# Scan products and low parts inside the passes, three attention steps for a pair of heads

## What is computed

```python
h = rmsnorm(x, norm_mix_w); proj = h @ w_in                # columns: z, xBC, dt, q, k, v, f
xbc = silu(causal_dwconv(xBC)); y_ssm = ssd_chunked(...)   # 16 heads of 64, 4 chunks of 128
y_ssm = rmsnorm(y_ssm * silu(z), ssm_norm_w)
q, k = rmsnorm per head; log_f = log_sigmoid(f + bias)     # 16 attention heads of 64
y_att = rmsnorm(forgetting_attention(q, k, v, log_f))      # causal, 4 blocks of 128 queries
x = x + concat(y_ssm, y_att) @ w_out
x = x + hierarchical_moe(rmsnorm(x))                       # 32 experts, top 1 group, top 2 in it
```

## Time and profile before

| | before |
|---|---|
| median of 3 runs | 728.06 us (727.43 to 728.72) |
| the profiled execution | 728.84 us |
| its span, first to last instruction | 727.1 us |
| mean granted TensorE clock, share of 2.4 GHz | 0.977 |
| busy: PE, DVE, ACT, POOL | 681.2, 392.7, 292.3, 148.9 us |
| moved by DMA | 162.78 MB |
| passes 20 to 35, window 137.12 to 264.00: PE busy, DVE busy | 123.67, 102.22 of 126.88 us |
| passes 44 to 51, window 304.70 to 418.10: PE busy, DVE busy | 109.89, 83.23 of 113.40 us |

### The profile page before, as it was taken

One profiled execution on the slowest core, in us unless ns is written; L12 is line 12 of the kernel. 1 busy time (PEld: TensorE's weight loads), 2 busy tenths in 40 slices (PEclk: granted clock), 3 DMA queues, 4 the chain that ended last, 5 costly groups with the idle time before them and its releaser, 6 DMA issues.

```text
span 727.1 us, 10707 instructions
## 1 busy us (share of the span) xinstructions
PE 681.2 (94%) x3850; PEld 467.0 (64%) x3850; DVE 392.7 (54%) x850; ACT 292.3 (40%) x659; POOL 148.9 (20%) x178
## 2 busy tenths in 40 slices
PE   8999999999999999999989999989999978887984
PEld 7878888777777888766656788877434323332542
DVE  6865778778879647777787654471222211121221
ACT  5934533564554636655665433221212111121200
POOL 2300010123312120012342142010132331122331
PEclk9999999999999999999999999989999989999998
DMA  8333345416346243290020069699999999999993
GB/s 295 101 106 116 98 152 162 132 70 174 112 121 170 63 146 117 78 356 1 30 88 1 3 226 421 257 368 355 409 420 415 404 411 402 420 419 414 416 397 109
DMA packets 61160, 162.78 MB, mean 224 GB/s; under 512 B 14184, under 2 KB 25604, under 8 KB 49840
## 3 DMA queue, kind: packets, MB, share of 16 engines
q1 hardware_dynamic: 49120, 144.64, 53.3%
q0 software_dynamic: 6880, 9.02, 4.2%
q10 hardware_dynamic: 5104, 8.39, 3.1%
HBM read 157.67 MB, written 20.28 MB: 245 GB/s over the span
## 4 chain that ended last, share of the span: by engine, by line
PE 31%; SPq 18%; DMA 3%; DVE 2%; issue 2%; ACT 1%; POOL 0%; POOLq 0%; DVEq 0%; ACTq 0%
SPq L401 6%; SPq L435 6%; SPq L449 5%; PE bank L1779 4%; PE bank L1373 4%; PE bank L1375 4%; PE bank L1374 4%; PE bank L1601 3%; DMA s_dn<-in_w_expert_down_dram 3%; PE bank L1808 3%; PE bank L1586 3%; PE bank L1577 2%; PE bank L1750 2%; SPq L443 1%; PE bank L1644 1%
## 5 line engine op out<-in xcount | busy, mean ns | idle before, releaser
L1779 PE MATMUL bank<-s_gu,s_xgT 128*64 128x512 f32 x352 | 84.7, 637 | 18.2 <-DMA s_gu<-in_w_expert_up_dram 18.2
L281 DVE TENSOR_TENSOR s_wl<-s_raw,s_wh 128x512 fp32r<-128x512 f32 x105 | 91.1, 913 | 11.9 <-ACT s_wh L994 11.5
L994 ACT ACTIVATE s_wh<-s_raw 128x512 fp32r<-128x512 f32 x120 | 72.8, 628 | 41.7 <-DMA s_raw<-in_w_in_dram 17.8
L1373 PE MATMUL bank<-s_wh,s_hTh 128*128 128x512 f32 x192 | 78.7, 410 | 0.0
L1779 PEld LDWEIGHTS bank<-s_gu,s_xgT 128*64 128x64 f32 x352 | 28.8, 146 | 73.2 <-issue 73.2
L1375 PE MATMUL bank<-s_wh,s_hTl 128*128 128x512 f32 x192 | 75.2, 391 | 0.0
L1374 PE MATMUL bank<-s_wl,s_hTh 128*128 128x512 f32 x192 | 74.8, 390 | 0.0
L1289 ACT ACTIVATE s_sg<-bank,s_slot_scale 128x256 f32<-128x256 f32 x16 | 7.6, 475 | 150.6 <-PE bank L1779 115.5
L1808 PE MATMUL bank<-s_dn,s_hidT 128*64 128x512 f32 x256 | 58.7, 599 | 2.0 <-DVE s_hidT L2347 1.6
L2347 DVE COPY s_hidT<-bank 128x256 f32<-128x256 f32 x16 | 6.8, 424 | 96.0 <-PE bank L1788 96.0
L2380 DVE SCALAR_TENSOR_TENSOR s_yrow<-bank,s_slot_scale,s_xg 128x512 f32<-128x512 f32 x30 | 21.2, 747 | 47.1 <-PE bank L1808 47.1
(11 more groups left out here) (307 smaller groups left out, 1402.3 us busy)
## 6 DMA issues: line engine op xcount, KB each, us to landing
s_dn<-in_w_expert_down_dram SPq DMA_DIRECT2D x28, 1024.0 KB, 28.9
s_gu<-in_w_expert_gate_dram SPq DMA_DIRECT2D x26, 1024.0 KB
s_gu<-in_w_expert_up_dram SPq DMA_DIRECT2D x24, 1024.0 KB, 28.8
s_raw<-in_w_in_dram SPq DMA_DIRECT2D x88, 256.0 KB, 4.0
s_raw<-in_w_out_dram SPq DMA_DIRECT2D x32, 256.0 KB, 3.7
s_gu<-in_w_expert_up_dram SPq DMA_DIRECT2D x12, 512.0 KB
s_decay_rows<-decay_rows SPq DMA_DIRECT2D x4, 1024.0 KB, 4.7
s_gu<-in_w_expert_gate_dram SPq DMA_DIRECT2D x8, 512.0 KB
```

The costliest lines, as they stand in the source:

```text
L281: eng.tensor_tensor(low, full, high.bitcast(F32), ALU.subtract).then_inc(sem(f"{what}_low_{low_engine(what, i)}"), 1)
L994: act.activation(wh[:, i % HL, :], raw[:, i % RAW, :], ACT.Copy).then_inc(sem("w_high"), 1)
L1373: pe.matmul(dst, ah, bh, start=start, stop=False)
L1779: last = pe.matmul(ps[j][r, :].rearrange("p (w f) -> p w f", w=2), m["xgT"][:, j, k, r], gu[:, half, :, k, :], start=(k == 0), stop=(k == ...
```

## The change

It has two parts. In the scan, `cb(0)` stands behind tile 4 of pass 21 instead of tile 1; `diag(c, 0)` and `diag(c, 1)` behind tiles 2 and 4 of the chunk's third pass instead of 1 and 3; `diag(c, 2)` and `diag(c, 3)` behind tiles 1 and 3 of the fourth pass instead of together ahead of it. The seven lows that VectorE made behind `y_add(c, 1)` are split: one ahead of `y_add(c, 1)`, three behind it, one between `qk_sum` and `qk_scale` of the fourth pass, two behind `state_keep`. In the attention, the last two query blocks of a pair (256 and 128 keys) become one step: 24 steps (`NEV`), with two row blocks in one bank, one P tile and one store, and still 54 tiles to spread them over.

```diff
-T_QK, T_P, T_END = T_X + 18, T_X + 34, T_X + 98
+T_QK, T_P, T_END = T_X + 18, T_X + 34, T_X + 82
...
+NEH = 3
+NEV = NEH * NHP
...
-    first, end = ((max(0, i) * NSTEP + 53) // 54 for i in ((n - N_SO) * KC + k, (n - N_SO) * KC + k + 1))
+    first, end = ((max(0, i) * NEV + 53) // 54 for i in ((n - N_SO) * KC + k, (n - N_SO) * KC + k + 1))
...
+        def steps_of(e):
+            hp, part = divmod(e, NEH)
+            return (TC * hp + part,) if part < NEH - 1 else (TC * hp + part, TC * hp + part + 1)
+        def spot(v):
+            step, par = divmod(v, 2)
+            hp, back = divmod(step, TC)
+            return 2 * (NEH * hp + min(back, NEH - 1)) + par, 2 * P if back == TC - 1 else 0
...
-                    if i == 1 and k == 1:
+                    if i == 1 and k == 4:
                         cb(0)
-                    if i >= 2 and i % 4 == 2 and k in (1, 3):
-                        diag(i // 4, k // 2)
+                    if i >= 2 and i % 4 == 2 and k in (2, 4):
+                        diag(i // 4, k // 2 - 1)
+                    if i >= 2 and i % 4 == 3 and k in (1, 3):
+                        diag(i // 4, 2 + k // 2)
...
                 if step == 1:
                     if c:
                         y_off(c, 1)
-                    diag(c, 2)
-                    diag(c, 3)
...
-            def p_transpose(step):
-                for v in (2 * step, 2 * step + 1):
+            def p_transpose(e):
+                for u in (2 * e, 2 * e + 1):
+                    pe.wait_ge(sem("p_scaled"), units_of(u)[-1] + 1)
...
             for i in range(16):
+                late = [r for r in slots_after(N_QK + i - 1)[4:] if low_engine("w", r) == "dve"] if i % 4 == 3 else []
                 qk_sum(i)
+                if late:
+                    weight_low(dve, late[0])
                 qk_scale(i)
...
                 if i % 4 == 2:
+                    soon = [r for r in slots_after(N_QK + i)[:4] if low_engine("w", r) == "dve"]
+                    for r in soon[:1]:
+                        weight_low(dve, r)
                     y_add(c, 1)
+                    for r in soon[1:]:
+                        weight_low(dve, r)
                 if i % 4 == 3 and c < TC - 1:
                     state_keep(c, 0)
                     state_keep(c, 1)
-                lows_after(N_QK + i)
+                for r in late[1:]:
+                    weight_low(dve, r)
+                if i % 4 != 2:
+                    lows_after(N_QK + i)
...
-                        if s + 2 < NSTEP:
-                            row_max(2 * s + 4)
-                            row_max(2 * s + 5)
+                        ahead = steps_of(s + 2) if s + 2 < NEV else ()
+                        if ahead:
+                            row_max(2 * ahead[0])
+                            row_max(2 * ahead[0] + 1)
                         pt_store(2 * s + 1)
-                        if s + 1 < NSTEP:
+                        if len(ahead) > 1:
+                            row_max(2 * ahead[1])
+                            row_max(2 * ahead[1] + 1)
+                        if s + 1 < NEV:
                             p_scale(s + 1)
```

More of the change, by code:

```diff
@@ L1567, in y_sums @@
                 last.then_inc(sem("sums_done"), 1)
-            def scores(step):
-                pair = (2 * step, 2 * step + 1)
-                for v in pair:
-                    h, hp, qb, n = unit(v)
-                    if v >= 3:
-                        pe.wait_ge(sem("max_known"), v - 2)
-                    r = slice((h % 2) * HD, (h % 2 + 1) * HD)
-                    pe.matmul(ps[4 + v % 3][:, 0:n], qT[r, hp, qb * P:(qb + 1) * P], kT[r, hp, 0:n], start=True, stop=True)\
-                        .then_inc(sem("s_done"), 1)
@@ L1580, in p_transpose, with scores @@
-            def p_transpose(step):
-                for v in (2 * step, 2 * step + 1):
-                    h, hp, qb, n = unit(v)
-                    pe.wait_ge(sem("p_scaled"), v + 1)
-                    t_read(pe, T_P + v - 2)
-                    for kb in range(qb + 1):
-                        last = pe.transpose(tbank(T_P + v)[:, kb * P:(kb + 1) * P], p_tile(v)[:, kb * P:(kb + 1) * P], ident[:])
+            def scores(e):
+                for step in steps_of(e):
+                    for v in (2 * step, 2 * step + 1):
+                        h, hp, qb, n = unit(v)
+                        u, off = spot(v)
+                        if u >= 3 and off == 0:
+                            pe.wait_ge(sem("max_known"), units_of(u - 3)[-1] + 1)
+                        r = slice((h % 2) * HD, (h % 2 + 1) * HD)
+                        pe.matmul(s_bank(v), qT[r, hp, qb * P:(qb + 1) * P], kT[r, hp, 0:n], start=True, stop=True)\
+                            .then_inc(sem("s_done"), 1)
@@ new lines, in p_transpose @@
+            def p_transpose(e):
+                for u in (2 * e, 2 * e + 1):
+                    pe.wait_ge(sem("p_scaled"), units_of(u)[-1] + 1)
+                    t_read(pe, T_P + u - 2)
+                    for v in units_of(u):
+                        h, hp, qb, n = unit(v)
+                        off = spot(v)[1]
+                        for kb in range(qb + 1):
+                            last = pe.transpose(tbank(T_P + u)[:, off + kb * P:off + (kb + 1) * P], p_tile(v)[:, kb * P:(kb + 1) * P], ident[:])
@@ L1624, in _ @@
                     if n == N_AO - 1 and k == 0:
-                        pv(NSTEP - 1)
+                        pv(NEV - 1)
             def x2_transpose(c):
```

127 lines of the change are left out of this document (71 added, 56 removed).

## The result

| | before | after |
|---|---|---|
| median of 8 runs each | 728.84 us (727.43 to 730.52) | 732.00 us (730.78 to 734.49) |
| the profiled execution, its span | 728.84, 727.1 us | 731.53, 729.8 us |
| tile 2 of pass 20 to the first score product | 154.54 us | 164.12 us |
| first score product to the first product of pass 52 | 131.56 us | 125.33 us |
| pass 52 to the end | 303.88 us | 303.15 us |

The ratio is 1.0048, 95% interval [1.0031, 1.0065]: slower by half a per cent, 3.2 us on the medians. The two halves of the change are six and ten microseconds of opposite sign. (The stages are distances between starts in the timeline of TensorE: tile 2 of pass 20 starts at 137.12 before and 137.20 after, the first score product at 291.66 and 301.32, pass 52 at 423.22 and 426.65. The first two tiles of pass 20 stand ahead of it, from 135.40 and 135.48; they are the same 1.72 us in both.)

What follows compares the result with a forecast made beforehand. TensorE's own stream bounds it up to the end of attention, the experts' weight stream after. +2.4 - 2.7 + 7.3 + 3.0 - 3.0 - 1.1 - 1.1 = +4.8 us on 728.06 gives 732.9 us, range 722 to 737.5.

Steps and rivals of the forecast that it cites:

- part 1: Scan, TensorE: moving `diag(c,2)` and `diag(c,3)` into pass 23+4c adds turns, 0.6 us in each of four chunks, +2.4 us.
- part 2: Scan, TensorE: of 3.2 us of waits on the scan's operands that the change aims at, 2.7 go, -2.7 us.
- part 3: Scan, VectorE: low parts come late under GpSimd's holds, so TensorE waits at tile 7, +7.3 us over four chunks.
- part 4: TensorE's clock: the long waits of chunks 1 and 0 each bring a fall of 1.5 us, +3.0 us.
- part 5: Attention: three steps for four save eight turns at 0.38 us each, -3.0 us.
- part 6: Attention waits: 1.1 us on `s_PT` goes, and 1.1 of 3.4 us around pass 47, clock fall included.
- one to three clock falls: The main forecast case, 732.9 us with that many falls of TensorE's clock; chance 0.47.
- The 1.1 us on `s_PT` goes: Attention, within part 6: the wait vanishes because step 1 comes one tile later with wider scores, -1.1 us.
- The lows are in time: Rival, scan: low 6 is ready at S+13.5 and no tile waits; 722.6 us, or 720 with pass 47 cleared; chance 0.26.
- The clock doesn't fall: Rival, scan: all waits as forecast, but each too short to lower TensorE's clock; 729.9 us, chance 0.17.
- the signs: Expected in the changed profile: `s_wl` waits, VectorE idle before `y_add(c,1)`, no `s_y` or `s_qn` wait, passes 44 to 51 shorter.
- The attention gives little: Rival, attention: turning costs only 1.6 us and pass 47 keeps its waits and clock fall; 735.4 us, chance 0.10.

Runs made afterwards that it cites:

- the small gate: Changed kernel with GpSimd's `gate` multiplying only 8 of its 1024 columns; total not comparable, scan 154.3 us against the changed kernel's 164.1.
- the lows ahead of it: Changed kernel with the last two late lows ahead of `state_keep` instead of behind it; 724.2 us, ratio 0.9954.
- `diag` together: Changed kernel with `diag(c,2)` and `diag(c,3)` back together ahead of pass 23+4c, the new order of the lows kept; 726.9 us, ratio 0.9984.
- the old order of the lows: Changed kernel with VectorE's order from before the change, TensorE's products still moved; 729.8 us, ratio 1.0022.
- the scores apart: Kernel with split lows and `diag(c,2)`, `diag(c,3)` together (720.9 us), with each merged step's 128-key scores in their own turn a tile later; 729.2 us.
- the first run: Changed kernel with its scan put back as before, leaving only the three attention steps for four; 721.8 us, ratio 0.992.
- gate late: Changed kernel with GpSimd's `gate` waiting until VectorE has made the last of the seven lows; 732.2 us, ratio 1.004.

## Why the prediction was right, point by point

The forecast was 732.9 us, slower, by lows that come late; the median is 732.0. The mechanism held, but that the two numbers are 0.9 apart is partly luck. The forecast added 4.8 us to a median of 728.06; over eight runs that median is 728.84, and the change is +3.2 (the spans of the profiled executions give +2.7). The sum was thus 1.6 us too large: it had one fall of the clock too many (1.4 us), took 1.0 us too little for the attention, and took the part from pass 52 on as unchanged, where it is 0.7 us shorter. A term that it left out, the time that a wait costs beyond what is listed, made good a part of that. Term by term (in the profiled executions):

| step of the prediction | forecast | measured |
|---|---|---|
| part 1, more turns | +2.4 | +0.59 in chunk 1 (17.60 us from pass 26 to pass 28 against 17.01), +0.62 in chunk 3 |
| part 2, waits of the scan removed | -2.7 | 3.2 listed before, 0.7 after: -2.5 |
| part 3, low parts late | 1.9, 3.3, 1.7, 0.4 | 2.0, 3.2, 1.7, 0.3 |
| part 4, clock falls in the scan | +3.0 (two) | +1.6 (one: pass 29 took 6.77 us, 5.32 before, and the small products ahead of it 0.96, where they took 0.80 in chunk 2) |
| scan in all | +10.0 | +9.6 |
| part 5, three steps for four | -3.0 | -3.4 (8 turns of 0.42) |
| part 6, waits of the attention | -2.2 | -2.8 (what is left of the 6.2) |
| attention in all | -5.2 | -6.2 |

**Part 3** was the step that set the sign, and it holds in its mechanism and in each of its sizes. The chain was S+6.5 for the end of `y_add`, S+12.1 for the fourth low, S+17.3 for the sixth. With S = 190.15 the trace has 196.73, 202.40 and about 207.7: S+6.6, S+12.3, S+17.6. That `gate` is what holds is shown by the small gate, that `state_keep` decides the end by the run with the lows ahead of it. What the prediction said too simply is that the moved `diag` makes it so. The run with `diag` together shows waits of 4.3 us from the order alone. The causes don't add: the full `gate`, the two lows behind `state_keep` and the place of `diag(c,2)` and `diag(c,3)` are worth 9.8, 6.6 and 4.0 us of scan, each taken away alone, out of 10.2 in all. Below the instant at which the tile is asked for, time on VectorE costs nothing; above it all of it counts.

These rows also bear on the page SBUF — State Buffer of the Trainium skill, section "Who interferes with whom". By its rule a low that has begun holds `gate` back, and with that time added to `gate`'s row the sum would have been 734.9. In the changed kernel the low begins at 196.65 and `gate` at 196.81, 0.08 us after `y_add` ends, and its row says 2.73 us, where the prediction's said 2.78. So nothing was added to its row. That the low does hold it, but within the row, can be read from `scaled_x` in the kernel before:

```profile
147.97 1.90 POOL L737 TENSOR_TENSOR s_Xs<-s_X,s_dte 128x1024 f32<-128x1024 f32 x1 [15.90 <-DVE s_dte L2088]
...
166.87 2.43 POOL L737 TENSOR_TENSOR s_Xs<-s_X,s_dte 128x1024 f32<-128x1024 f32 x1 [1.08 <-PE bank L1527]
```

At 147.97 no operation of VectorE is running, at 166.87 a low has just begun and has 0.67 us to go, and the same work takes 0.53 us more. Elsewhere it is in between, with less left of the low (2.00 us with 0.24 left in the kernel before, 2.12 with 0.36 in the changed one). The page's rule holds here, and the prediction was right to count the delay as contained in `gate`'s 2.78, for that row was taken under a low too. On another point also the page and this trace agree: a copy on VectorE is held as well, the one at 161.89 takes 1.51 us under the select where its like takes 0.43.

**Part 4** was sized wrong: two falls at +3.0, where one came, worth 1.6. The wait of 1.8 us in chunk 0, like that of 1.7 in chunk 2, left no mark; the one of 3.2 did. Of the forecast case, "one to three clock falls", it was the lower end. One reading under this part was wrong: no slice of the granted clock among the first 26 of the earlier trace rows is under nine tenths (the page has an 8 in the 21st slice of TensorE's busy share, not of its clock), and a slice of 18 us can't show such a fall, for 1.7 us of lost work leave it at 0.91. So neither the slices before, nor the two that the forecast wanted to see below full in the scan, of which there is none, decide anything; the windows do. Nor did the step by which the falls were counted hold, that a single wait does what two that are as long together did: the 1.8 us of chunk 0 left the clock full, where two waits of 1.25 and 0.66 us (the old order of the lows) brought a fall.

What stood against it was a term that I had left out: each wait costs some 0.3 us beyond what is listed. In chunk 1 pass 28 with the transposes behind it took 10.53 us against 6.93, 0.38 more than its wait of 3.22 (0.16 of it is the lower clock), and in chunk 2 8.63 against 6.69, 0.24 more than its 1.70. With 0.65 for the two waits of chunk 0 (9.32 us against 6.66 in the small gate's run, 2.01 listed) and 0.47 in chunk 3 (6.74 against 5.93, 0.34 listed) that is 1.7 us over the five new waits, less about 0.3 for each of those that went.

**Part 5**: a pair of heads without waits takes 2.61 + 1.95 + 2.17 + 2.40 = 9.13 us from the last product before a turn to the first behind it, in its four turns before (384.89 to 397.05), and 3.04 + 2.61 + 2.83 = 8.48 in three now (386.55 to 397.51); with 0.23 for each turn's product taken off, 0.42 us for each turn saved. 0.38 was forecast. The price of a bare turn is 0.30 by the run with the scores apart; the rest probably belongs to the products of a step that are no longer begun on their own, which no run tested.

**Part 6** failed in one step: "The 1.1 us on `s_PT` goes". It stayed in another form. Before, the distance from that score product to the P·V was 1.76 us with 0.42 of work in it, now it is 1.79 with 1.05: a loss of 0.7 where it had been 1.3, unlisted since part of it lies within the group of scores. So about 0.6 went of the 1.1. The cause is the same row maximum behind three lows. Pass 47 gave more than I took: of the 2.2 us of waits from there to the first tiles of pass 48, 0.75 stay, and the fall of the clock (1.4 us of work) is gone. I had kept too much, afraid that larger steps on a full VectorE would wait as long. A wait of 0.5 us for the last merged step is new.

**The rivals.** "The lows are in time" is what two of the runs (the small gate, the lows ahead of `state_keep`) then nearly made true by other means, and 722.6 for it was about right (724.2 with the lows ahead of the state). "The clock doesn't fall" was half so. Of the signs, the waits of 1.9, 3.3 and 1.7 us came as 2.0, 3.2 and 1.7, and the idle time before `y_add(1,1)` as 1.69; `s_y` is gone, but 0.4 us on `s_qn` stays, and passes 44 to 51 are 6.2 us shorter, not 4. "The attention gives little" fell with the first run.

## What to carry to other kernels

Before work is moved on one engine, write down for the engine that it feeds when each item is ready and when it is asked for, with the holds by a neighbour in it. Here two lows behind four operations on the state turned a gain of some 4 us into a loss of 3, and the same lines the other way round give it back. Such a chain has a threshold: below it extra microseconds are free, above it each costs one, and more with the 0.3 us of starting again and the clock. A gap must be looked for as a distance between starts too, since many small ones, or one inside a group, stand in no table of waits.

## What the runs showed of the hardware

- TensorE's granted clock fell to the lower level at single waits of 3.2, 2.2 (diag together), 2.0, 2.0 and 3.9 us (gate late), and at two of 1.25 and 0.66 us whose ends lay 1.3 us apart (old order of the lows); it stayed full after single waits of 1.8, 1.7 and 1.3 us. When it fell was not the same each time: 1.45 us after the wait's end in the changed kernel, 0.03 (diag together), and 0.69, 0.11 and 0.63 (gate late), in all these with the engine at work again; in the kernel before it fell inside the second of two waits. Each fall cost 1.6 to 1.8 us of work (1 - 0.89 of 16 us is 1.8; the granted clock is 0.50 from 209.3 to 212.7, which is 1.7).
- A pass with a listed wait is 0.24 to 0.47 us longer than the wait says (chunks 2 and 3 of the changed kernel; 0.29 with the small gate). Some 0.28 of it can be seen in the rows: the idle time is counted from the end of a product's 0.40 us, where the next would have started after 0.23, and the first one behind starts its successor later (207.84 to 208.18, 0.34 against 0.23).
- GpSimd held, beside the lows, an operation on the state (1.83 us instead of 0.69, small gate) and a copy (1.51 instead of 0.43), each with its inputs in SBUF. Operations that take one input from a bank were not seen longer under it than without it (`y_add`'s first, 0.68 us under the select at 189.82 in the kernel before and 0.68 without).
- A low part that is already running holds GpSimd in turn, and the time is inside the row of GpSimd's instruction: `scaled_x` takes 1.90 us alone and 2.43 when a low has 0.67 us to go.
